# Four tiles of the value projection moved into the block of q's and k's norms

## The reference, cut to what matters

```python
mod = jnp.dot(jax.nn.silu(c), w_mod[l]) + b_mod[l]
shift1, scale1, gate1, shift2, scale2, gate2 = jnp.split(mod[:, None, :], 6, axis=-1)
h = rms_norm(x, g_norm1[l]) * (1.0 + scale1) + shift1
proj = jnp.dot(h, w_in[l])
x_lru, z_lru, q, k, v = jnp.split(proj, SPLITS, axis=-1)
...
y_att = diff_attention(q, k, v, g_q[l], g_k[l], lam, g_attn_out[l], rel_bias, lam_init)
```

## Time and profile before

| what | us |
|---|---|
| median of 3 timed runs | 2144.35 (2143.42 to 2146.89) |
| the profiled execution: its own time | 2155.99 |
| its span in the trace | 2154.2 |
| TensorE busy | 2075.5 (96%) |
| VectorE busy | 1664.9 (77%) |
| ScalarE busy | 1083.4 (50%) |
| GpSimd busy | 235.8 (11%) |

### The profile page before, as it was taken

The page is one execution under the profiler, slowest core; times in us unless marked ns, Lnnn a source line. Parts: engine busy times, 40 slices in busy tenths (PEclk is TensorE's granted clock), DMA queues, the critical chain, the costliest instruction groups (busy, mean ns, idle before and its releaser), DMA issues. The chain is left out here.

```text
span 2154.2 us, 25217 instructions
## 1 busy us (share of the span) xinstructions
PE 2075.5 (96%) x9978; PEld 1611.3 (75%) x9978; DVE 1664.9 (77%) x1714; ACT 1083.4 (50%) x1241; POOL 235.8 (11%) x171
## 2 busy tenths in 40 slices
PE   6999999999998999999999979999999999999998
PEld 4767855777865888888888757888888875588876
DVE  5575226896568999999999768999999978854776
ACT  4388135885135777777777543112122168523143
POOL 0200010001001011110110140000000014233040
PEclk9999988999999999999999979999999999999999
DMA  8311143004268999999999751111122155433121
GB/s 290 111 40 40 40 163 117 1 1 91 92 234 352 409 393 393 402 393 402 393 402 393 259 187 42 59 59 51 67 79 98 50 173 195 170 127 117 40 79 59
DMA packets 131715, 380.17 MB, mean 176 GB/s; under 512 B 9559, under 2 KB 25231, under 8 KB 131620
## 3 DMA queue, kind: packets, MB, share of 16 engines
q1 hardware_dynamic: 117828, 338.85, 41.3%
q0 software_dynamic: 7568, 23.09, 4.4%
q10 hardware_dynamic: 6224, 16.93, 2.0%
HBM read 335.72 MB, written 43.06 MB: 176 GB/s over the span
## 5 line engine op out<-in xcount | busy, mean ns | idle before, releaser
L2691 DVE SCALAR_TENSOR_TENSOR arena<-arena,vecs 128x1023 f32<-128x1023 f32 (+14 forms) x240 | 304.3, 1268 | 7.1
L2273 DVE TENSOR_TENSOR w_low<-W,w_high 128x2048 fp32r<-128x2048 f32 x96 | 216.7, 2286 | 30.5 <-ACT w_high L2001 26.6
L1643 PE MATMUL Q<-hT_high,w_high 128*128 128x512 f32 (+1 forms) x736 | 230.4, 392 | 1.8 <-DVE hT_low L2256 1.0
L2273 DVE TENSOR_TENSOR w_low<-arena,w_high 128x2048 fp32r<-128x2048 f32 x96 | 218.3, 2289 | 17.6 <-ACT w_high L2001 17.6
L1643 PE MATMUL Q<-hT_low,w_high 128*128 128x512 f32 (+1 forms) x720 | 225.3, 391 | 0.0
L2001 ACT ACTIVATE w_high<-arena 128x2048 fp32r<-128x2048 f32 x96 | 184.2, 1920 | 74.0 <-PE Q L1844 74.0
L1643 PE MATMUL Q<-hT_high,ring_low 128*128 128x512 f32 x704 | 220.3, 390 | 0.0
L2001 ACT ACTIVATE w_high<-W 128x2048 fp32r<-128x2048 f32 x96 | 184.0, 1919 | 67.8 <-PE Q L1844 61.2
L1656 ACT ACTIVATE w_high<-W 128x1024 fp32r<-128x1024 f32 x44 | 46.5, 1058 | 251.8 <-PE Q L1643 243.0
L1844 PE MATMUL Q<-w_high,x_high 128*128 128x512 f32 x528 | 164.4, 393 | 1.9 <-ACT x_high L2019 1.2
L1844 PE MATMUL Q<-w_low,x_high 128*128 128x512 f32 x528 | 162.6, 389 | 0.0
(11 more groups left out here) (497 smaller groups left out, 4154.2 us busy)
## 6 DMA issues: line engine op xcount, KB each, us to landing
W<-in_w_dram SPq DMA_DIRECT2D x48, 2048.0 KB, 17.2
arena<-in_w_dram SPq DMA_DIRECT2D x48, 2048.0 KB, 17.2
W<-in_w_mod_dram SPq DMA_DIRECT2D x12, 2048.0 KB, 9.8
W<-in_w_in_dram SPq DMA_DIRECT2D x11, 2048.0 KB, 8.9
W<-in_w_out_dram SPq DMA_DIRECT2D x6, 2048.0 KB, 9.2
spill<-arena ACTq DMA_DIRECT2D x24, 512.0 KB, 2.7
W<-in_w_in_dram SPq DMA_DIRECT2D x10, 1024.0 KB, 9.4
W<-cs_rows SPq DMA_DIRECT2D x11, 512.0 KB, 5.0
```

Of the source, the lines that this page charges most:

```text
L1643: ins = nc.tensor.matmul(Q[rows, 2 * pair_of(n) + half, :], w[:, k], x[:, k, HALF * half:HALF * half + HALF], start=k == 0 and w is high a ...
L2273: nc.vector.tensor_tensor(wl[:], chunk_src(r, j), wh[:].bitcast(F32), ALU.subtract).then_inc(low_v, 1)
L2691: ins = nc.vector.scalar_tensor_tensor(conf[:, i, j:], u[:, 0:S - j], w, conf[:, i, j:], ALU.mult, ALU.add)
```

## The change

The first block now projects tiles 0 to 3 of the values (`V_FIRST` = 4) into banks 0, 2, 4 and 6, and ends its ScalarE order with squares 0 and 1. Tiles 4 to 7 are projected in the second block into banks 0 to 3 (`value`), one before the lambda product, one behind sums 0 and 1, one behind 2 and 3, one behind 4 and 5 and the first modulation product. Bias products and the first two `next_vector` come behind all sums. Since `h1_low` is still read for tokens 512 to 1023, what the second block keeps in tiles 0 to 7 goes into their lower halves: the inverse roots' parts are cut in two (`qk_parts[0]` and `[1]`), `qk_high` moves to tile 7, `qk_spread` to tile 1, and the buffers of the squares to tiles 15 and 33. The table of the bias is negated in place and read with a stride of zero, instead of being spread into a tile of its own. ScalarE's `part(0)` waits for the last value tile; its second `y_first` waits for the second `low_rows`.

```diff
+        V_FIRST = NT // 2
+        def v_bank(t):
+            return Q[:, 2 * t if t < V_FIRST else t - V_FIRST, :]
+        square_of = [tiles(15), tiles(33)]
...
-                send_units(sync, U_GATE1 + NU)
+                send_units(sync, U_V + NU)
...
-                for t in range(NT):
+                for t in range(V_FIRST):
                     n = 32 + t
...
+                act.wait_ge(v_done, lru_level[STEPS - 1])
+                for n in range(2):
+                    nc.scalar.activation(square_of[n], qk[:, n], ACT.Square).then_inc(sq_ready, 1)
...
                 def near():
                     pe.wait_ge(hot_in, 16)
                     pe.wait_ge(table_ready, 1)
+                    pe.wait_ge(proj_v, NLRU + NT)
                     for h in range(HEADS):
-                        nc.tensor.matmul(Q[:, h, :], table_bc[:, h], hot, start=True, stop=True).then_inc(near_mm, 1)
-
-                mod_product(pe, unit(pe, U_GATE1), 5)
+                        nc.tensor.matmul(Q[:, h, :], table_h[0:NB, h:h + 1].broadcast_to((NB, P)), hot,
+                                         start=True, stop=True).then_inc(near_mm, 1)
+
+                def value(t):
+                    at = slice(P * t, P * t + P)
+                    for k in range(KD):
+                        _, w_high, w_low = v_parts(k // 2)
+                        for x, w in ((h1_high, w_high), (h1_low, w_high), (h1_high, w_low)):
+                            ins = nc.tensor.matmul(v_bank(t), x[:, k, at], w[:, k % 2],
+                                                   start=k == 0 and x is h1_high and w is w_high,
+                                                   stop=k == KD - 1 and w is w_low)
+                    ins.then_inc(proj_mm, 1)
+
+                value(V_FIRST)
...
                 sums(0)
                 sums(1)
-                next_vector(0)
+                value(V_FIRST + 1)
                 sums(2)
                 sums(3)
-                near()
+                value(V_FIRST + 2)
                 pe.wait_ge(mask_ready, 1)
                 sums(4)
                 sums(5)
-                next_vector(1)
+                mod_product(pe, unit(pe, U_GATE1), 5)
+                value(V_FIRST + 3)
                 sums(6)
                 sums(7)
+                near()
+                next_vector(0)
+                next_vector(1)
                 pe.wait_ge(near_ready, HEADS)
...
                     if i:
                         act.wait_ge(row_mm, i)
+                    else:
+                        act.wait_ge(proj_mm, 32 + NT)
...
-                square(0)
-                square(1)
...
-                part(0)
                 square(2)
                 square(3)
...
-                added(0)
-                part(1)
-                root(0)
                 square(4)
                 square(5)
+                root(0)
                 high_rows(0)
                 square(6)
                 square(7)
+                part(0)
+                root(1)
+                high_rows(1)
+                added(0)
+                part(1)
                 added(1)
                 part(2)
-                root(1)
                 act.wait_ge(near_mm, HEADS)
-                for m in range(2):
-                    y_first(m)
-                high_rows(1)
+                y_first(0)
                 added(2)
                 part(3)
                 far(0)
+                act.wait_ge(parts_low, 2)
+                y_first(1)
                 added(3)
                 part(4)
...
+                value_copy(V_FIRST)
                 dve.wait_ge(lam_e, 1)
...
+                value_copy(V_FIRST + 1)
                 invert(0)
+                value_copy(V_FIRST + 2)
+                dve.wait_ge(sign_ready, 1)
+                low_rows(0)
+                value_copy(V_FIRST + 3)
+                invert(1)
                 for h in range(HEADS):
                     dve.wait_ge(near_mm, h + 1)
                     nc.vector.tensor_copy(bias_near[h], Q[:, h, :]).then_inc(near_ready, 1)
-                dve.wait_ge(sign_ready, 1)
-                low_rows(0)
-                norm(0)
-                invert(1)
-                for n in range(1, HEADS):
+                for n in range(HEADS):
                     norm(n)
```

More of the change, by code:

```diff
@@ L393, in wait_low @@
                 pe.wait_ge(in_low_ready, f + 1 - sum(g < f for g in POOL_LOW))
+        square_of = [tiles(15), tiles(33)]
+        sq_ready = sem("sq_ready")
         proj_mm = sem("proj_mm")
@@ L596, in _ @@
                         at = slice(P * t, P * t + P)
-                        ins = three(Q[:, 2 * (n % 4), :], h1_high[:, k, at], h1_low[:, k, at],
+                        ins = three(v_bank(t), h1_high[:, k, at], h1_low[:, k, at],
                                     high[:, k % 2], low[:, k % 2], k == 0, k == KD - 1)
@@ L732, in _ @@
                     in_rest(FEATURES + p)
-                for t in range(NT):
-                    n = 32 + t
-                    dve.wait_ge(proj_mm, n + 1)
-                    nc.vector.tensor_copy(v_sb[:, t], Q[:, 2 * (n % 4), :]).then_inc(proj_v, 1)
+                for t in range(V_FIRST):
+                    dve.wait_ge(proj_mm, 32 + t + 1)
+                    nc.vector.tensor_copy(v_sb[:, t], v_bank(t)).then_inc(proj_v, 1)
             @block.scalar
@@ L837, in _ @@
                     in_first(FEATURES + f - 4 - STEPS)
+                act.wait_ge(v_done, lru_level[STEPS - 1])
+                for n in range(2):
+                    nc.scalar.activation(square_of[n], qk[:, n], ACT.Square).then_inc(sq_ready, 1)
         hot = tiles(6)[0:NB, 0:HALF]
-        table_bc = tiles(7)[0:NB, 0:HEADS * P].rearrange("b (h p) -> b h p", h=HEADS)
         bias_near = [tiles(14 + h // 2)[:, HALF * (h % 2):HALF * (h % 2) + HALF] for h in range(HEADS)]
@@ L847, in program @@
         lam_ready, lam_mm, lam_e = sem("lam_ready"), sem("lam_mm"), sem("lam_e")
-        sq_ready, sum_mm, root_q, qk_normed = sem("sq_ready"), sem("sum_mm"), sem("root_q"), sem("qk_normed")
+        sum_mm, root_q, qk_normed = sem("sum_mm"), sem("root_q"), sem("qk_normed")
         VECS = 2 * HEADS
@@ L859, in program @@
         sign = tiles(5)[:, 1:2]
-        qk_spread = rounded("qk_spread", 4, [P, 2, HEADS, P])[:, 1]
-        qk_parts = rounded("qk_parts", 3, [P, S])
-        qk_high = rounded("qk_high", 2, [P, 4, QUARTER])
+        qk_spread = rounded("qk_spread", 1, [P, HEADS, P])[:]
+        qk_parts = [rounded(f"qk_parts{half}", t, [P, HALF]) for half, t in enumerate((3, 0))]
+        qk_high = rounded("qk_high", 7, [P, 2, QUARTER])
         qk_lower = tiles(5)[:, P:P + QUARTER]
@@ L918, in _ @@
                            [[-2, HEADS], [0, REPEAT], [1, VECS]], 0)
-                nc.gpsimd.memset(qk_parts[:].bitcast(F32), 0.0).then_inc(masks, 1)
+                g_link(nc.gpsimd.memset(qk_parts[0][:].bitcast(F32), 0.0))
+                nc.gpsimd.memset(qk_parts[1][:].bitcast(F32), 0.0).then_inc(masks, 1)
                 for h in range(HEADS):
@@ L954, in sums @@
                         ins = nc.tensor.matmul(Q[32 * q:32 * q + 32, sum_bank[g], 0:QUARTER], qk_sum[:, b, 0:32],
-                                               tiles(n % 2)[:, QUARTER * q:QUARTER * q + QUARTER],
+                                               square_of[n % 2][:, QUARTER * q:QUARTER * q + QUARTER],
                                                start=b == 0, stop=b == HEADS - 1)
@@ L965, in spread @@
                     for half in range(2):
-                        ins = nc.tensor.matmul(Q[:, 2 * (n % 2) + half, :], qk_spread[:, b],
-                                               qk_parts[:, HALF * half:HALF * half + HALF], start=True, stop=True)
+                        ins = nc.tensor.matmul(Q[:, 2 * (n % 2) + half, :], qk_spread[:, b], qk_parts[half][:],
+                                               start=True, stop=True)
                     ins.then_inc(spread_mm, 1)
@@ L1020, in square @@
                         act.wait_ge(sum_mm, n - 1)
-                    nc.scalar.activation(tiles(n % 2), qk[:, n], ACT.Square).then_inc(sq_ready, 1)
+                    nc.scalar.activation(square_of[n % 2], qk[:, n], ACT.Square).then_inc(sq_ready, 1)
                 def root(g):
@@ L1043, in high_rows @@
                     act.wait_ge(rows_inv, g + 1)
[L1044 to L1047 removed]
+                    nc.scalar.activation(qk_high[:, g], qk_rows[:, g], ACT.Copy).then_inc(parts_high, 1)
                 nc.scalar.activation(tiles(5)[:, DK:P].rearrange("p (o e) -> p o e", e=VECS),
@@ L1087, in _, with value_copy @@
             def _(dve):
-                for h in range(HEADS):
-                    ins = nc.vector.tensor_scalar_mul(table_bc[:, h], table_h[0:NB, h:h + 1].broadcast_to((NB, P)), -1.0)
-                ins.then_inc(table_ready, 1)
+                def value_copy(t):
+                    dve.wait_ge(proj_mm, 32 + t + 1)
```

(5 more changed lines are left out.)

1 line of the change is left out of this document (removed).

## The result

The changed kernel takes 2156.62 us (median of 6 runs, 2150.9 to 2160.49), against 2143.89 (2141.8 to 2146.89) for 6 runs of the kernel before beside it: a ratio of 1.0056, with an interval of 1.0041 to 1.0071. It is slower, by 12.7 us, and outside the predicted range. The prediction named this outcome as rival B, with a chance of 0.19.

A forecast was written before the change was run, and what follows sets the result against it. TensorE, busy 96% of the span, and its granted clock were taken as the bound. Full-clock work and lost clock gave −8.2 + 8.0 = −0.2 on 2144.35, so 2144.0 us, range 2137.5 to 2150.5.

The forecast's parts named there:

- rival B: Second block's tail: clock stays low for four of five row and modulation product pairs, +8.3, 2152.6 us; chance 0.19.
- the two prices of the block: Second block, TensorE's stage: its time is its instructions at full clock, 45.7 us, plus what the clock costs.
- Steps 1 to 5 and 8: Value tiles, mask wait, squares, copies, first modulation product, third weight unit: nothing, but −0.7 for masks and 0 to 0.1 for copies.
- step 1: Four value tiles leave the first block (−21.76) for the second (+21.76), 5.44 us each: net zero.
- step 8: Third unit of modulation weights, requested at 298.1 after the last value tile: 14.5 us of cover against 8.5 or 12, nothing.
- Step 6: Two next_vectors back to back in the second block: nothing covers ScalarE's copy any more, +0.8 us.
- Step 7: ScalarE's second y_first waits for parts_low 2 and delays row product 4: +0.4 us at full clock, nothing at half.
- Full-clock sum, +0.5: Second block with its value tiles counted at full clock: 68.0 us, ending at 338.4; the change itself +0.5.
- Clock cost 8 in the new order: Second block: half clock behind the bias products and once in the old tail, 5.6 to 9.6 us, taken as 8.
- It took 54.4. The clock cost 8.7: Second block before the change: 45.7 us at full clock against 54.4 taken, so 8.7 us of clock cost.
- Differences inside the stage carry over: The profile's −0.2 us was applied to the timed median 2144.35, 11.6 lower than the profiled 2155.99.
- I take it unchanged, and give it ±2 for the range: Attention's start: its low stretch (351.5 to 362.0 at 0.51) was assumed to stay, with ±2 us.

The follow-up runs named there:

- e6: Changed kernel with the four value tiles in a lump at the second block's start, then the order of before: 2148.1 us, ratio 1.0004 to before.
- e8: The kernel before, unchanged, one more profiled execution: 2145.95 us.
- e11: e6 with the first vector moved behind the fourth sum and the bias products, straight ahead of the first row product: 2159.6 us, ratio 1.006 to before.
- e10: e9 with the seventh sum ahead of the first row product and the eighth behind the first vector: 2150.5 us, ratio 1.0017 to before.
- e9: Changed kernel with the bias products moved between the first modulation product and the last value tile: 2151.7 us, ratio 1.0015 to before.
- e7: Changed kernel with row product 0 and modulation products 0 and 1 between value tiles, bias behind the last sums: 2151.5 us, ratio 1.0013 to before.

## Why the prediction was wrong

- *What bounds the kernel; the two prices of the block*: right. TensorE is as busy as before, and the clock decides.
- *Steps 1 to 5 and 8, at nothing*: nearly right. There is no wait but the block's start until 311, and none on weights; e6 (1.0004) shows no cost of all of it together that could be measured. But a value tile among the sums takes 5.65 to 5.71 us from start to start of what follows, not 5.44: step 1's net zero was +0.9. In step 8 the sum is 298.0, not 298.1, which changes nothing.
- *Step 6, the bubble of 0.8*: 0.72. *Step 7, +0.4*: the row product starts 1.12 behind its spreads instead of 1.03, so 0.1, under the bound.
- *Full-clock sum, +0.5*: near. From the last value copy of the first block to the attention, without half of the low time and without the moved tiles, before has 45.2, 45.8 and 45.3 us in its three profiles (55.43 − 10.2, 49.2 − 3.4, 50.4 − 5.1), after 54.71 − 8.5 = 46.2.
- *Clock cost 8 in the new order*: right for the execution profiled: 17.1 us low, which cost half of it, 8.5. The two places, behind the bias products and once in the old tail, were right too.
- *The step that failed: "It took 54.4. The clock cost 8.7", and then "Differences inside the stage carry over".* The 8.7 us of before came from one execution, and this one lay at the slow end: 2155.99, where 82 of 95 others are under 2154. The prediction saw the 11.6 us to the median and put them outside the stage. The runs showed that most of them were clock, half of it in the stage: by the mean clocks (0.9806 in the timed runs, 0.976 in the profile) about 0.0046 × 1730 = 8 us. Against e8, a typical execution, the profiled one had 5.0 us more in the block, 3.2 more in the attention's scores and 2.1 more in the first block. So the sum "−8.2 + 8.0" gives back a cost that the base of 2144.35 mostly didn't hold. With e8's 5.1 us of clock cost in the block (half of its 10.2) the stage comes to +0.5 + 8.0 − 5.1 = +3.4, and 4.3 is what after's profile shows.
- *The second term that failed: the attention's start, "I take it unchanged, and give it ±2 for the range".* It is low for 10 to 14 us in 12 of 14 profiles and not in e8 and e11. From its first to its last score product the attention takes 145.6 us without it and 148.8 to 150.6 with it, so the ±2 should have reached to −5. Both profiles of after have it, e8 does not, and this is 4.9 of the 10.6 us between e8 and after. Whether the new order makes it more frequent can't be told from so few profiles.
- *Rival B* fell on the right side for a reason other than its own. It had the clock low through four of five pairs; the profiles of the changed kernel show three low stretches in the block, 17.1 and 13.7 us together, so 7 to 8.5 us of cost, which is the forecast's own figure. The time came from before being better than its profile, not from after being worse than forecast. That its 2152.6 is nearer the measured 2156.6 is luck.

The Trainium skill (TensorE: Matmul & The Clock Gate, What's actually happening) says that the clock's history differs from run to run of one kernel, because the chip's observation isn't aligned with the kernel. The traces agree: three profiles of one kernel, three patterns. The same section holds the warm-up penalty to be below 1% of a typical span and not worth fitting. That is said of the start, and here the low stretches lie all through the kernel: 102.7 us of low time in before's profile cost about half of it, an estimated 51 us or 2.4%. From one execution to another the time moves by 0.9% (2138 to 2157 us), and an order of work shifted its mean by 0.43%, the whole effect in question.

What stays open: why the order without the waits costs 4 to 7 us, that is, which length or make-up of thin work brings a fall, how often, and how long it lasts. Equal instructions fell in e10 and not in e9, so this would need many profiles of each order, not one. None of the orders tried is measurably faster than the kernel before; four with the tiles in the block (e6, e7, e9, e10) are the same as it within what can be told.

## What to carry to other kernels

Before a price is taken from a profile, hold the profiled execution against the timed ones: time and mean clock both. If it lies at an end of their spread, its clock losses are not the kernel's typical ones, and a difference computed against it must be corrected by the slope of time on clock. And when work is regrouped on TensorE, take the order of thin and dense products for a cost of its own, even where no instruction is added: compare orders by the times and mean clocks of many executions, since one profile of each shows falls that the next one may not have.

## What was not expected of the hardware

- One program, unchanged, takes 2138 to 2157 us, and 0.001 of mean granted clock goes with 1.73 us (correlation −0.96 over 95 executions).
- The block's own products can run wholly at 1.00 (e6, 290.0 to 333.25, busy 43.25 of 43.25 us), and a dense value tile can run almost wholly at 0.50 (e10, 294.25 to 301.0). Neither the busy share nor the kind of product at that moment fixes the clock.
- In nine of fourteen profiles the clock falls while the four bias products run (32 of 128 rows in use, about 3.7 us at full clock), with different work before and behind them.
- The low stretch at the attention's start is not tied to the attention: it was absent in two of fourteen profiles, and there 3 to 5 us were saved.
